# Output projection of a mixer layer: six of its eight weight blocks computed beside the attention units and stored as partial sums

## The chip, the cores and the metric

The kernel runs on one core of one Trainium2 chip. The metric is the device time of one execution in microseconds; the kernel before took 2520.68 us (median of three runs, 2518.25 to 2520.77). The profiled execution is another one and took 2515.9 us.

## The reference

One layer of a hybrid trunk for 2048 prompt rows and 64 sample rows (T = 2112 rows of 1024 numbers). Four mixers A to D give 256 columns each. Their outputs are normalised, scaled, projected by `w_out`, gated by `g1` and added to `x`; then come a second norm and a mixture of experts. What the change touches is this part:

```python
mix = jnp.concatenate([out_a, out_b, out_c, out_d], axis=-1).reshape(Bn, L, N_MIXERS, W_GRP)
mix = (mix * lax.rsqrt(jnp.mean(mix * mix, axis=-1, keepdims=True) + EPS)).reshape(Bn, L, D) * p['out_norm']
x = x + (g1 * (mix @ p['w_out']))
h2 = _rms(x, p['norm_ffn']) * (1.0 + sc2) + sh2
x = x + (g2 * _moe(h2, p))
```

`out_d` is the attention of the prompt (two patterns whose results are merged by a softmax of their maxima and sums) and of the samples; `out_a` to `out_c` are finished earlier and lie, normalised and turned, in `mix_d`. `w_out` has eight blocks of 128 rows: blocks 0 to 5 belong to A to C, blocks 6 and 7 to D. `g1` is one row for the whole prompt and one row for each of the eight samples.

## The kernel before, in words

All engines walk one list, `SCHEDULE`; each engine has a function for some of the step names and executes them in the order of the list. Rows are taken in 17 tiles of 128 (the last has the 64 sample rows).

**The first part** (to 796 us) computes the norms, the input projection, mixers A to C, and q, k and v. A barrier, `("bar", 1)`, ends it.

**The attention units.** There are 128 units: 32 blocks of queries times four heads. `BLOCKS` goes by chunks of 512 rows: for each chunk 16 units of the band pattern (two key blocks of 128; the very first query block has one) and 16 of the dilated one (1, 2, 3 and 4 key blocks in chunks 0 to 3). That is 284 key blocks in all. Slot u of the list holds, in this order (`unit`): `ao` of u-3 (DVE copies a finished block), at even u the pair `au` of u and u+1 (TensorE scores, line 2230, DVE maximum, line 1715, ACT exponential, line 1159), `at` of u-1 (transposes, line 2238, into bank 2 or 3 by parity, copied by DVE at even and by ACT at odd units), `ap` of u-2 (times v, line 2249). `sample(u)` adds the sample attention (lines 2269 to 2299) beside units 3 to 55; its keys and values come by POOL's queue, lines 833 and 838.

**The row steps.** From slot 48 on each slot u has one step of the row tiles too, `tiles(i, j)` with i = (u-48)//8 - 2 and j = (u-48)%8, so that the first projection stands beside unit 64 and the tiles run on after unit 127. A tile has eight such steps:

```python
out = [[("pe", i - 1, 1), ("x", i - 1), ("m1", i + 1)],
       [("m2", i + 1), ("l", i - 2), ("mx", i + 1), ("xt", i)],
       [("m3", i + 1)],
       [("n3", i - 1)],
       [("pe", i, 0), ("ma", i + 2), ("st", i - 1)],
       [("mo", i + 1)],
       [("t", i - 1, 0)],
       [("t", i - 1, 1)]][j]
out = [("p", i, j // 4, j % 4)] + out
```

`p` is a quarter of half a projection: two matmuls of 128x512 (line 2326, bank 5 or 6), 16 to a tile. `pe` (DVE, line 1830) multiplies the half by the gate, `x` adds the input row (DVE, 1836) and squares the sum for the second norm (ACT, 1214 to 1216), `n3` norms it (DVE, 1845 and 1846), `t` turns it (TensorE 2336, ACT 1222), `l` gives the router's logits (2344, 2345). `m1`, `m2` and `m3` merge the two patterns for the tile ahead and norm it (DVE 1785 to 1820, with an exponential on ACT, 1188, between m1 and m2, and a root on ACT, 1194, between m2 and m3); `mo` turns the merged rows. SP's queue loads `mx` (mix_d), `xt` (x) and `ma` (att_d) and stores `st`. Router steps r0 to r4 (DVE mostly) run for four tiles at a time, each batch in the slots `ROUTE` gives; POOL then scatters the rows' places (line 881, ten of them after the last two batches).

**The experts** follow (`moe`): 32 experts' weights come by SP's queue, 2 MB each for `wg`, `wu` and `wd`. Expert 0 is loaded in step `pre` at tile 9, expert 1 in step `w1` after the last tile.

## Time and profile before

| what | value |
| --- | --- |
| median of three runs | 2520.68 us |
| the profiled execution | 2515.9 us, its span 2514.2 us |
| TensorE busy | 2240.9 us (89%) |
| DVE, ACT, POOL busy | 852.5, 550.3, 286.1 us |
| mean granted clock of TensorE | 0.933 of full |

### The profile page before, as it was taken

Reading aid. Unit: us, or ns where it says so; the run is one execution under the profiler, and the core shown is the slowest. Engines: PE = TensorE matmul, PEld = TensorE weight load, DVE = VectorE, ACT = ScalarE, POOL = GpSimd, SP = SyncE. Lnnn points to the kernel's source line nnn. Section 1 sums busy time; section 2 is a strip of 40 time slices with the busy share of each in tenths; the row PEclk is TensorE's granted clock in tenths of the full one; section 3 lists DMA queues with packets and bytes.
Section 4 is the critical chain, followed back from the end, with each engine's and each line's share of the span. In section 5 each row is a group of like instructions: output and inputs, shape, how many; then the busy total and the mean of one; then the engine's idle time right before and its main releaser. Section 6 shows DMA issues by size and latency. Waiting matters only on the chain. (4 is left out here: it accounts for less than half of the span.)

```text
span 2514.2 us, 27705 instructions
## 1 busy us (share of the span) xinstructions
PE 2240.9 (89%) x7615; PEld 1121.0 (45%) x7616; DVE 852.5 (34%) x1969; ACT 550.3 (22%) x1061; POOL 286.1 (11%) x460
## 2 busy tenths in 40 slices
PE   4996999998895778999999849999999999999993
PEld 1343555444452444555554424444444444444441
DVE  4575642036541233445466431111111111111211
ACT  3410101235531322333322201111111111111111
POOL 0001011000001000000021121111111111111211
PEclk8998999999997777999999969999999999999997
DMA  9152131333547424222163245675658789687962
GB/s 378 71 214 48 57 86 48 140 101 99 169 144 242 158 108 174 67 78 85 61 233 131 81 163 156 216 275 170 211 190 326 260 329 343 206 307 278 323 200 59
DMA packets 106523, 438.90 MB, mean 175 GB/s; under 512 B 14955, under 2 KB 53579, under 8 KB 85883
## 3 DMA queue, kind: packets, MB, share of 16 engines
q1 hardware_dynamic: 76160, 309.46, 32.9%
q0 software_dynamic: 26160, 113.16, 16.5%
q10 hardware_dynamic: 4112, 15.14, 1.5%
q8 instruction: 48, 0.79, 0.1%
q14 instruction: 43, 0.35, 0.0%
HBM read 356.39 MB, written 83.10 MB: 175 GB/s over the span
## 5 line engine op out<-in xcount | busy, mean ns | idle before, releaser
L2410 PE MATMUL bank<-arena 128*128 128x512 f32 x1120 | 492.8, 596 | 14.6 <-issue 14.5
L2098 PE MATMUL bank<-arena 128*128 128x512 f32 (+1 forms) x960 | 358.3, 533 | 9.6 <-ACTq L1003 9.6
L2410 PEld LDWEIGHTS bank<-arena 128*128 128x128 f32 x1120 | 212.4, 190 | 291.0 <-issue 291.0
L2326 PE MATMUL bank<-arena 128*128 128x512 f32 (+1 forms) x544 | 267.8, 626 | 0.0
L2438 PE MATMUL bank<-arena 128*128 128x512 f32 x560 | 250.4, 600 | 9.0 <-issue 8.8
L2098 PEld LDWEIGHTS bank<-arena 128*128 128x128 f32 x960 | 168.5, 191 | 193.5 <-issue 192.8
L1990 DVE COPY arena<-bank 128x512 f32<-128x512 f32 x50 | 34.6, 693 | 549.1 <-PE bank L2425 549.1
L2438 PEld LDWEIGHTS bank<-arena 128*128 128x128 f32 x560 | 103.6, 190 | 133.0 <-issue 129.9
L2326 PEld LDWEIGHTS bank<-arena 128*128 128x128 f32 (+1 forms) x544 | 97.5, 195 | 88.4 <-issue 87.9
L2249 PE MATMUL bank<-arena 128*128 128x64 f32 x568 | 95.6, 302 | 31.1 <-DVEq L1733 17.3
L2198 PE MATMUL bank<-arena 128*128 128x512 f32 (+1 forms) x272 | 121.6, 600 | 0.0
L2000 DVE TENSOR_TENSOR arena<-bank,arena 128x512 f32<-128x512 f32 (+1 forms) x50 | 34.5, 691 | 255.9 <-PE bank L2438 208.2
L916 POOL DMA_INDIRECT o_y<-arena x50 | 79.3, 1586 | 301.3 <-DVE arena L2002 215.1
L1715 DVE CUSTOM_DVE_ANT_0 arena<-bank,arena 128x256 f32<-128x256 f32 (+3 forms) x128 | 58.3, 455 | 159.6 <-PE bank L2230 126.3
L1159 ACT ACTIVATE arena<-arena 128x256 f32<-128x256 f32 (+3 forms) x128 | 68.3, 533 | 201.5 <-DVEq L1717 193.6
L2249 PEld LDWEIGHTS bank<-arena 128*128 128x128 f32 x568 | 87.3, 222 | 44.0 <-ACTq L1170 23.3
L2414 PE MATMUL bank<-arena 128*64 128x512 f32 x224 | 99.2, 594 | 6.1 <-issue 5.3
L2415 PE MATMUL bank<-arena 128*64 128x512 f32 x224 | 99.3, 595 | 0.0
L1255 ACT COPY arena<-bank 128x512 f32<-128x512 f32 x52 | 30.6, 588 | 305.3 <-PE bank L2376 305.3
L1041 ACT COPY arena<-bank 128x512 f32<-128x512 f32 (+1 forms) x50 | 25.6, 513 | 314.8 <-PE bank L2098 314.6
L2230 PE MATMUL bank<-arena 64*128 64x256 f32 (+3 forms) x256 | 72.4, 648 | 9.2 <-SPq L440 9.2
L2238 PE MATMUL bank<-arena 128*128 128x128 f32 x284 | 64.4, 321 | 15.2 <-ACTq L1161 15.1
(453 smaller groups left out, 2502.5 us busy)
## 6 DMA issues: line engine op xcount, KB each, us to landing
arena<-wg SPq DMA_DIRECT2D x32, 2048.0 KB
arena<-wu SPq DMA_DIRECT2D x32, 2048.0 KB, 15.1
arena<-wd SPq DMA_DIRECT2D x32, 2048.0 KB, 8.4
arena<-mod_w SPq DMA_DIRECT2D x12, 2048.0 KB, 18.1
z_d<-arena ACTq DMA_DIRECT2D x12, 1056.0 KB, 6.6
arena<-z_d POOLq DMA_DIRECT2D x10, 1056.0 KB, 8.3
arena<-kc POOLq DMA_DIRECT2D x8, 1280.0 KB, 7.6
arena<-vc POOLq DMA_DIRECT2D x8, 1280.0 KB, 8.1
```

The source lines that it names most:

```text
L916: pool.indirect_dma_start(out=O["y"], out_offset=bass.IndirectOffsetOnAxis(ap=sidx[:, s:s + 1], axis=0), in_=yb[:, s], in_offset=None, com ...
L1159: link(act.activation(ssb[:, u % 4, 0:w], ssb[:, u % 4, 0:w], ACT.Exp, bias=ost[:, (u // 4) % 2, u % 4, 64:65], scale=-1.0, accum_out=ost[ ...
L2098: ins = mm(bank[n % 2][:, 0:w], wz[:, i % 3, k, :], hT[:, k, t0:t0 + w], start=(k == 0), stop=(k == KT - 1))
L2198: mm(bank[i % 3][0:r], hT[:, k, t0:t0 + r], wqkv[:, k, 0:512], start=(k == 0), stop=(k == KT - 1))
L2230: mm(bank[u % 2][:, 0:128 * len(vt)], qkT[rr, h // 2, q], qkT[rr, 2 + h // 2, k], start=True, stop=True).then_inc(S("att_s"), 1)
L2238: ins = pe.transpose(bank[2 + u % 2][:, c * P:(c + 1) * P], ssb[:, u % 4, c * P:(c + 1) * P], ident)
L2249: ins = mm(bank[4][:, 64 * h:64 * h + 64], pt[:, u % 4, c * P:(c + 1) * P], v[:, t, 64 * h:64 * h + 64], start=(c == 0), stop=(c == len(vt ...
L2326: ins = mm(bank[5 + q][0:r], l, wo[:, k, 512 * q:512 * q + 512], start=(k == 0), stop=(k == KT - 1))
L2410: ins = mm(bank[bk][:, :], xgT[:, s, k, :], m[w][:, k, :], start=(k == 0), stop=(k == KT - 1))
L2414: gate = mm(bank[2][HIGH, :], xgT[:, s, k, LOW], wg[w][:, k, :], start=(k == 0), stop=(k == KT - 1), tile_position=(0, HB))
L2415: rise = mm(bank[3][LOW, :], xgT[:, s, k, LOW], wu[w][:, k, :], start=(k == 0), stop=(k == KT - 1), tile_position=(0, 0))
L2438: ins = mm(bank[4 + h][:, :], hhT[:, k, :], wd[w][:, k, 512 * h:512 * h + 512], start=(k == 0), stop=(k == 3))
```

## The change

`w_out`'s blocks 0 to 5 leave the row tiles. They become 34 "parts": for each half q of the columns (512) and each of the 17 row tiles, one chain of six matmuls into bank 3 (`part`, two halves of three matmuls, `("w", n, 0)` and `("w", n, 1)`), beside units 2 and 3, 6 to 37, 42 and 43, 46 to 77. Six blocks of weights (`WB`, 256 KB each) are loaded for q = 0 and again for q = 1. DVE scales them by the prompt's gate (`part_scale`, six operations of 128x512) after the sample part has used them unscaled, and adds the part to the row of x that SP has loaded (`part_add`, one operation of 128x512). SP stores the sum to `xp_d` and reads it back in `xt` in x's place. The transposes of units below 80 have bank 2 alone, so that each waits for the copy of the one before.

The row tiles start at unit 78, two steps to a slot while units are left (53 slots), one after that. A tile's projection keeps two matmuls to a half, with a weight scaled beforehand by the gate (`w2g`), and stands at j = 3 and j = 7. DVE takes bank times the row's root plus the stored row in one operation for each half; `x`'s addition and `m3` are gone, and the merged rows' square sum goes from DVE to ACT. The sample rows are tile 1 now instead of tile 16. `pre` stands at (12, 1) instead of (9, 5), and expert 1's `wu` is loaded only when all scatters have landed.

```diff
+        WFIRST = 2
+        ONEBANK = 80
...
+        NW = 2 * NT
+        WAT = [WFIRST + 40 * q + (2 * p + 2 if p else 0) for q in range(2) for p in range(NT)]
...
+        def later(u):
+            out = [("we", n) for n in range(NW) if WAT[n] + 2 == u]
+            return out + [("wsc", n // NT) for f, n in out if n % NT == 0]
+
+        def partial(u):
+            out = []
+            for n in range(NW):
+                if u in (WAT[n], WAT[n] + 1):
+                    out.append(("w", n, u - WAT[n]))
+                if u == WAT[n] and n + 1 < NW and n:
+                    out.append(("wl", n + 1))
+                if u == WAT[n] + 3:
+                    out.append(("wst", n))
+                    out += [("wi", m) for m in range(4, len(WITEMS)) if XI[n] <= m - 4 and (n + 1 == NW or m - 4 < XI[n + 1])]
+                if n == NT - 1 and u == WAT[n] + 2:
+                    out.append(("ww", 1))
+            return out
+
         def unit(u):
-            pair = [("au", u), ("au", u + 1)] if u % 2 == 0 else []
+            pair = [("au", u), *((f, n) for f, n in later(u)), ("au", u + 1)] if u % 2 == 0 else []
...
-                   [("m2", i + 1), ("l", i - 2), ("mx", i + 1), ("xt", i)],
-                   [("m3", i + 1)],
+                   [("m2", i + 1), ("l", i - 2), ("xt", i)],
+                   [],
...
-            out = [("p", i, j // 4, j % 4)] + out
...
+            out = ([("p", i, j // 4)] if j % 4 == 3 else []) + out
...
-            if (i, j) == (9, 5):
+            if (i, j) == (12, 1):
                 out.append(("pre",))
...
-        FIRST_ROW = 48
-        for u in range(FIRST_ROW + 8 * (NT + 4)):
-            i, j = divmod(u - FIRST_ROW, 8)
-            SCHEDULE += unit(u) + sample(u) + (tiles(i - 2, j) if i >= 0 else [])
+        FIRST_ROW = max(WAT) + 2
+        BOTH = NU + 3 - FIRST_ROW
+        for u in range(NU + 3 + 8 * (NT + 4) - 2 * BOTH):
+            SCHEDULE += unit(u) + sample(u) + partial(u)
+            n = u - FIRST_ROW
+            for g in (2 * n, 2 * n + 1) if n < BOTH else (n + BOTH,):
+                if g >= 0:
+                    SCHEDULE += tiles(g // 8 - 2, g % 8)
...
+            return bank[2 + u % 2 if u >= ONEBANK else 2][:, 0:w]
...
+                if m >= 4:
+                    f4, n4 = WITEMS[m - 4]
+                    if f4 == "x":
+                        sp.wait_ge(S(f"st_wx{m % 4}"), 16 * sum(1 for e in range(m % 4, m - 3, 4) if WITEMS[e][0] == "x"))
...
+            def part_out(step, n):
+                r, t0, m = w_rows(n), w_at(n), XI[n]
+                sp.wait_ge(S("w_out"), n + 1)
+                sp.dma_start(xp_d[t0:t0 + r, 512 * (n // NT):512 * (n // NT) + 512], xw[0:r, m % 4]).then_inc(S(f"st_wx{m % 4}"), 16)
...
-                sp.dma_start(xt[0:r, i % 2], A["x"][t0:t0 + r]).then_inc(S(f"ld_xt{i % 2}"), 16)
+                sp.dma_start(xt[0:r, i % 2], xp_d[t0:t0 + r]).then_inc(S(f"ld_xt{i % 2}"), 16)
...
+                sp.wait_ge(S("st_tok"), 16 * 2 * NT)
+                weights_of(1, None, ("wu",))
...
+                    link(TT(x, bank[3][0:r], x, ALU.add))
+                    dve.sem_inc(S("w_free"), 1)
...
-                link(TT(x1[0:r, i % 2, c], bank[5 + q][0:r], g[0:r, 0, c], ALU.mult))
+                    link(STT(y, bank[5 + q][0:r], rstd, x, ALU.mult, ALU.add))
...
-            def x1_sum(step, i):
...
-                link(TT(x1[0:r, i % 2], x1[0:r, i % 2], xt[0:r, i % 2], ALU.add))
...
+                if 0 < u <= ONEBANK:
+                    pe.wait_ge(S("att_ptV" if u % 2 else "att_ptA"), (u - 1) // 2 + 1)
...
+            def part(step, n, half):
+                r = w_rows(n)
+                if half == 0:
+                    pe.wait_ge(S(f"ld_mix{n % 2}"), 16 * (n // 2 + 1))
+                    if n:
+                        pe.wait_ge(S("w_free"), n)
...
+                    ins = mm(bank[3][0:r], mixl[:, n % 2, k, 0:r], WB[k], start=(k == 0), stop=(k == 5))
```

**TensorE beside unit 18 to 21, before.** Scores (2230), transposes (2238), times v (2249) and the samples' values (2297):

```order
L2230 MATMUL bank0<-arena 128x128
L2230 MATMUL bank1<-arena 128x128
L2238 MATMUL bank3<-arena 128x128
L2249 MATMUL bank4<-arena 128x64
L2297 MATMUL bank7<-arena 32x256 x8
L2238 MATMUL bank2<-arena 128x128
L2249 MATMUL bank4<-arena 128x64
L2297 MATMUL bank7<-arena 32x256 x8
```

The same place of the changed kernel (scores 2360, transposes 2372, times v 2383, samples 2431, parts 2458):

```order
L2360 MATMUL bank0<-arena 128x128
L2360 MATMUL bank1<-arena 128x128
L2372 MATMUL bank2<-arena 128x128
L2383 MATMUL bank4<-arena 128x64
L2431 MATMUL bank7<-arena 32x256 x8
L2458 MATMUL bank3<-arena 128x512 x3
L2372 MATMUL bank2<-arena 128x128
L2383 MATMUL bank4<-arena 128x64
L2431 MATMUL bank7<-arena 32x256 x8
L2458 MATMUL bank3<-arena 128x512 x3
```

Each unit has got three matmuls of 512 columns behind its own work, and both transposes go to bank 2.

**TensorE in the row tiles beside units of three key blocks, before.** One projection step (2326) to a unit, here with `mo` (2310) and `t` (2336):

```order
L2230 MATMUL bank0<-arena 128x384
L2230 MATMUL bank1<-arena 128x384
L2238 MATMUL bank3<-arena 128x128 x3
L2249 MATMUL bank4<-arena 128x64 x3
L2326 MATMUL bank6<-arena 128x512 x2
L2238 MATMUL bank2<-arena 128x128 x3
L2249 MATMUL bank4<-arena 128x64 x3
L2326 MATMUL bank6<-arena 128x512 x2
L2310 MATMUL bank7<-arena 128x128 x2
```

The changed kernel's tiles beside units of two key blocks (projection 2473, `mo` 2444, `t` 2482):

```order
L2473 MATMUL bank5<-arena 128x512 x2
L2360 MATMUL bank0<-arena 128x256
L2360 MATMUL bank1<-arena 128x256
L2372 MATMUL bank3<-arena 128x128 x2
L2383 MATMUL bank4<-arena 128x64 x2
L2444 MATMUL bank7<-arena 128x128 x2
L2372 MATMUL bank2<-arena 128x128 x2
L2383 MATMUL bank4<-arena 128x64 x2
L2482 MATMUL bank7<-arena 128x128 x4
L2473 MATMUL bank6<-arena 128x512 x2
L2482 MATMUL bank7<-arena 128x128 x4
```

A tile's projection is four matmuls instead of sixteen, and a tile passes in four units instead of eight.

**DVE in a row tile after the last unit, before** (1830 is `pe`, 1836 the addition of x, 1785 to 1787 `m1`):

```order
L1830 TENSOR_TENSOR arena<-bank6,arena 128x512
L1836 TENSOR_TENSOR arena<-arena 128x1024
L1785 TENSOR_TENSOR arena<-arena 128x4
L1786 TENSOR_TENSOR arena<-arena 128x4
L1787 TENSOR_TENSOR arena<-arena 128x4
```

The changed kernel's DVE in such a tile (1964 is `pe`, 1922 to 1924 `m1`, then the end of `m2`, and `n3` at 1975 and 1976):

```order
L1964 SCALAR_TENSOR_TENSOR arena<-bank6,arena 128x512
L1922 TENSOR_TENSOR arena<-arena 128x4
L1923 TENSOR_TENSOR arena<-arena 128x4
L1924 TENSOR_TENSOR arena<-arena 128x4
L1936 TENSOR_TENSOR arena<-arena 128x4
L1937 TENSOR_TENSOR arena<-arena 128x4
L1938 TENSOR_TENSOR arena<-arena 128x4
L1939 RECIPROCAL arena<-arena 128x4
```

```order
L1943 TENSOR_TENSOR arena<-arena 128x256
L1944 TENSOR_TENSOR arena<-arena 128x256
L1945 TENSOR_TENSOR arena<-arena 128x256
L1975 SCALAR_TENSOR_TENSOR arena<-arena 128x1024
L1976 TENSOR_TENSOR arena<-arena 128x1024
```

`m1` follows `pe` at once, and `n3` follows `m2` at once: the addition of 128x1024 and the norm that stood between `m2` and `n3` (1812, 1820) are gone.

## Rows read from the trace of the kernel before

**Rows 1.** The profile's page: span, and the granted clock in 40 slices.
```profile
span 2514.2 us, 27705 instructions
...
PEclk8998999999997777999999969999999999999997
```
**Rows 2.** Busy time by stretch: length, PE, PEld, DVE, ACT, POOL; then clock, DMA share, GB/s.
```profile
796.00:997.00 201.00, 146.29 (x772) 83.33 (x772) 61.53 (x216) 55.86 (x177) 25.10 (x48) 0.71 0.45 165
997.00:1262.00 265.00, 255.82 (x1108) 148.15 (x1109) 125.74 (x339) 92.87 (x254) 0.28 (x1) 0.94 0.21 73
1262.00:1430.00 168.00, 159.87 (x543) 81.60 (x542) 103.16 (x300) 38.82 (x108) 30.96 (x39) 0.97 0.44 155
1430.00:1486.00 56.00, 11.56 (x66) 9.55 (x67) 31.37 (x133) 6.78 (x19) 13.90 (x19) 0.53 0.52 180
```
**Rows 3.** Timeline of PE around unit 78: start, length, instruction, count, idle before.
```profile
1048.56 0.70 PE L2230 MATMUL bank<-arena 64*128 64x256 f32 x4
```
**Rows 4.** Timeline of PE in a row tile after the last unit.
```profile
1361.57 1.87 PE L2344 MATMUL bank<-arena 128*128 128x36 f32 x16
...
1363.71 7.13 PE L2326 MATMUL bank<-arena 128*128 128x512 f32 x16
1370.68 0.38 PE L2310 MATMUL bank<-arena 128*128 128x128 f32 x2
```
**Rows 5.** Timeline of PE over two units of two key blocks.
```profile
1145.36 0.70 PE L2230 MATMUL bank<-arena 64*128 64x256 f32 x4
...
1148.43 0.60 PE L2336 MATMUL bank<-arena 128*128 128x128 f32 x4
1148.87 0.38 PE L2238 MATMUL bank<-arena 128*128 128x128 f32 x2
...
1151.78 0.70 PE L2230 MATMUL bank<-arena 64*128 64x256 f32 x4
```
**Rows 6.** Groups of PE between 796 and 997: busy, mean ns, idle before.
```profile
L2269 PE MATMUL bank<-arena 128*32 128x512 f32 (+1 forms) x96 | 25.9, 670 | 11.4 <-issue 11.4
L2297 PE MATMUL bank<-arena 128*32 128x256 f32 x160 | 24.3, 450 | 6.2 <-DMA arena<-o_v 6.2
L2282 PE MATMUL bank<-arena 128*128 128x128 f32 x20 | 4.8, 377 | 0.0
```
**Rows 7.** Timeline at the start of the units: POOL and PE.
```profile
805.36 1.07 POOL L833 DMA_DIRECT2D arena<-kc  x2
...
815.24 3.63 PE L2269 MATMUL bank<-arena 128*32 128x512 f32 x8 [8.87 <-issue]
```
**Rows 8.** Timeline of DVE and ACT in a row tile after the last unit.
```profile
1357.90 0.69 DVE L1830 TENSOR_TENSOR arena<-bank,arena 128x512 f32<-128x512 f32 x1 [5.02 <-PE bank L2326]
1358.74 1.23 DVE L1836 TENSOR_TENSOR arena<-arena 128x1024 f32<-128x1024 f32 x1
1360.06 1.06 ACT L1214 ACTIVATE arena<-arena 128x1024 f32<-128x1024 f32 x1 [1.14 <-DVEq L1837]
1361.89 0.21 ACT L1188 ACTIVATE arena<-arena 128x8 f32<-128x8 f32 x1
1362.25 0.17 DVE L1799 TENSOR_TENSOR arena<-arena 128x4 f32<-128x4 f32 x1 [1.57 <-ACTq L1189]
1364.85 0.43 DVE L1812 CUSTOM_DVE_ANT_0 arena<-arena 128x256 f32<-128x256 f32 x1
1368.87 1.29 DVE L1845 SCALAR_TENSOR_TENSOR arena<-arena 128x1024 f32<-128x1024 f32 x1
1370.19 1.23 DVE L1846 TENSOR_TENSOR arena<-arena 128x1024 f32<-128x1024 f32 x1
```
**Rows 9.** Busy time by stretch again: row loads, and expert 0's weights.
```profile
1358.00:1364.00 6.00, 6.00 (x30) 3.99 (x29) 3.83 (x13) 2.45 (x6) 0.00 (x0) 1.00 0.60 199
1300.00:1320.00 20.00, 19.91 (x72) 10.49 (x70) 13.84 (x39) 5.05 (x13) 3.98 (x4) 1.00 1.01 402
```
**Rows 10.** DMA issues by line: KB each, median us to landing.
```profile
o_y<-arena SPq DMA_DIRECT2D x17, 512.0 KB, 2.7
```

305 lines of the change are left out of this document (196 added, 109 removed).

## The prediction

> **What bounds the kernel now.** I read the page first [rows 1]: one core, and TensorE's clock in forty slices. It is at 0.7 in four of them, and these lie beside the attention units. The busy times by stretch say what happens there [rows 2]. From 796 to 997 us stand units 0 to 63 alone: TensorE works 146 of 201 us, at a mean clock of 0.71, so it is neither full nor fast. From 997 to 1262 units 64 to 127 have row steps beside them, and TensorE is busy 256 of 265 us at 0.94. From 1262 to 1430 the row tiles are alone: 160 of 168 us at 0.97. The 56 us to 1486 are the router's last steps and the first gather, and TensorE works 12 of them. So TensorE bounds the two middle stretches, waits on the units' chain in the first, and what can be won is the first stretch's idle time and half clock. The rest of the kernel is not touched.
>
> **Prices, all at full clock.** Eight matmuls of 512 columns take from 1363.71 to 1370.68 [rows 4], so 0.87 us each. Two units of two key blocks with two row steps between take 6.42 us, 1145.36 to 1151.78; the steps are four such matmuls (3.48) and eight transposes (0.44 for four, 1148.43 to 1148.87) [rows 5]; 2.06 us are left, 0.515 to a key block. Of the 284 key blocks 136 belong to units 0 to 77 (70 us) and 148 to units 78 to 127 (76 us). The samples' three large groups are busy 55 us at a clock of 0.71 [rows 6, 2], so 39 us at full clock. A row tile is 16 matmuls (13.9), logits (2.1, 1361.57 to 1363.71 [rows 4]) and ten transposes (1.1): 17.1 us. The new tile has four matmuls: 6.7 us. As a check on such sums, 997 to 1262 holds 176 key blocks and 8.4 tiles, 91 + 144 = 235 us, and took 265: 0.47 us above the sum for each of its 64 units, half of it clock.
>
> **First stretch, units 0 to 77.** TensorE's work adds up to 204 matmuls x 0.87 = 178 us of parts, 70 of units and 39 of samples: 287 us. The waits per unit lie nearest to those of the stretch that also has matmuls beside units, so 78 x 0.47 = 37 us. At the start TensorE waits for the first keys, issued at 805.36 and used at 815.24 [rows 7]; of those 19 us since 796 the first four units and part 0 fill 9; SP's first loads (2.9 MB, 7 us at the 402 GB/s of [rows 9]) go partly ahead of the keys, 3 more: 13 us, and 2 for a spot named below, 15. The stretch ends at 796 + 287 + 37 + 15 = 1135, where unit 78 starts at 1048.56 now [rows 3]. Bounds: 1100 with no waits at all, 1170 with 1 us more for each part. DVE's 34 additions of 0.69 us and twelve scalings (0.69 each, the price of a 128x512 operation [rows 8]) are 32 us on an engine that was busy 62 of 201 us; they lie beside TensorE's work, except that TensorE may not begin a part before the last one's addition is read, which is in the 0.47. The part's matmuls also cover the chain score, maximum, exponential, transpose: 2.6 us of them stand between two units' transposes, and with one bank for these ACT's copy must be over before the next. Without a part in the slot (units 38 to 41, 44, 45) that cover is gone, up to 2 us a pair; before, all pairs went without it, so I add only 2 in all.
>
> **Second stretch, 53 slots with two row steps each.** TensorE has 76 us of units and 11.25 tiles x 6.7 = 75 us. With 0.47 us a slot that is 176 us. DVE is now as loaded: today's tile costs it 1.4 for two gates, 1.23 for the sum, 0.6 for `m1` (three like 1362.25), 2.6 for `m2` (1362.25 to 1364.85), 0.95 for square sum and norm, and 2.55 for `n3` (1368.87 to 1371.42): 9.3 us [rows 8]; 8.4 of these leave 48 of its 126 us [rows 2] for 64 units, 0.75 each. After the change a tile costs it 7.2 us, and 53 x 0.75 + 11.25 x 7.2 plus two batches of router steps (23: what 8.6 tiles of 9.3 leave of the 103 us in the stretch from 1262 [rows 2], which holds two) plus 4 for the gates is 148 us against TensorE's 151. Two engines so alike, each waiting on the other in order, do not reach 176. The other end is today's pace, 265 / 64 = 4.14 us a slot: 219 us. I take the middle, 197: the stretch ends at 1332.
>
> **Third stretch, tiles alone.** 46 steps are left up to the last projection, 5.75 tiles. TensorE would need 6.7 us a tile; what sets the pace is the ring through DVE and ACT: `pe` 0.75, ACT's turn with a copy ahead 0.4, squares and exponential to DVE's next 2.2 (1360.06 to 1362.25), `m2` 2.6, `n3` 2.55 [rows 8], hand-over 0.3, four transposes and the half projection behind them 2.5 [rows 4, 5]: 11.3 us. TensorE then works six tenths of the time. In the stretch where it worked 146 of 201 us the clock was 0.71 [rows 2]; at half clock the last term doubles and the ring is 13.6 us. I take 12.5 as the middle, 72 us. By the Trainium skill (TensorE: Matmul & The Clock Gate, "A second HAM failure mode: psum-queue depth-cycling"), small idle gaps between groups of matmuls make the clock go to and fro between its two rates; with the half rate held throughout, this stretch would be 78 us, with the full rate 65. The row just named agrees with such a to and fro. Router batch 2 adds about 11 us on DVE, 8 of them in the ring. Expert 0's 6.3 MB at 402 GB/s [rows 9] take 16 us of SP's queue; behind them the next merge rows have some 12 steps before they are due, so I add 3. Third stretch: 83 us, bounds 65 + 8 and 78 + 11 + 15.
>
> **The end.** 1332 + 83 = 1415 against 1430. The 56 us to 1486 lose the addition of 1.23 us [rows 8], and gain up to 5 us because expert 1's `wu` now loads together with the token table and the first gathers; expert 1 is wanted a good 20 us later, so only the contention counts: +1 net. The experts stay. In sum -14 us on the profiled execution of 2515.9 us, whose time is 4.8 us below the median of the runs shown: 2502 there, **2507 us** on the median's scale.
>
> **Rivals.**
> **Saturated.** The parts cover every wait of the units and keep the clock at 1.0, and DVE keeps up. Then the first stretch ends at 1118 (half the waits), the second takes 176 and the third 73: 1367, 63 us less than 1430, so 2459. For it: 256 of 265 us busy in the stretch that looks most like it. Against: 30 us were lost there even so, and DVE carries more per slot now.
> **DVE holds the tiles (slower).** A whole tile's DVE work falls into four units instead of eight: in the slot with `pe`, `m1` and `m2` DVE has 4.1 + 0.75 us against TensorE's 3.3, and the maximum of the next pair waits behind `n3`; so exponential, transposes and TensorE wait. Place: units 78 to 127 and every tile after. Price: the second stretch at today's 4.14 us a slot is 219, the third at the half-clock ring 78 + 11 + 8 = 97: 1135 + 219 + 97 = 1451, +21 and +2 at the end: 2543. It decides from the point where the two stretches together pass 1430 - 1135 = 295 us; my sum has 280. For it: the 148 against 151 above. Against: ACT has room (93 of 265 us), and the first eight slots have no projection.
> **Parts come late (slower).** SP stores a part, must see it landed before it loads that buffer's next x, and then comes to the next mixer rows. A store of 512 KB lands after 2.7 us [rows 10]; the row loads moved 1.2 MB in some 5 us [rows 9], so a mixer load of 384 KB lands about 4 us after its issue. Both fit in a part's 8.3 us. But 16 loads of 1.28 MB for the samples go through the same engines, 3 us each. One microsecond on each of 34 parts gives +34 - 14: 2541. By the Trainium skill (DMA: Bandwidth & Descriptors, "Anatomy of one DMA"), most of a transfer's fixed time of about 2 us is the wait for the last byte to be confirmed, longest when it goes to HBM; that speaks against partial sums that are stored and read back, and would cost 34 x 2 = 68 us if SP's queue were full. The store row agrees with the size; nothing in the trace before shows SP full.
> **Nothing in sum.** What the first stretch wins (the 1.0 clock and the filled gaps) the tiles give back within 5 us: 2516 to 2526, which my sum reaches if each of the three stretches is a few us longer. It is part of the first case below.
>
> **How the numbers follow.** My sum as it stands, scattering from 2490 to 2525: 0.42, of which 0.33 below 2515.6 and 0.09 within 0.2% (5 us, about what can be told from no change). Saturated 0.15, faster. DVE holds the tiles 0.24: 0.22 slower, 0.02 within. Parts late 0.13: 0.11 slower, 0.02 within. Smaller mixtures 0.06: 0.02 faster, 0.01 within, 0.03 slower. Faster 0.50, same 0.14, slower 0.36. The likeliest case alone spans 2490 to 2525; with both signs open the range runs from near the saturated case to the slower ones, 2465 to 2545.
>
> **What would show it.** Unit 78's scores should start at 1120 to 1150, with a clock above 0.9 from 830 on; if they start past 1165, look for TensorE waiting at a part's first matmul for a load (parts late) or at a transpose. The last unit should end at 1320 to 1345, the last projection at 1405 to 1430. DVE should be busy about three quarters of the second stretch; if TensorE's waits there name DVE's maximum or copies and a slot takes over 4 us, the DVE rival holds. In the third stretch a tile should take 12 to 13 us at a clock of 0.6 to 0.9; under 9 us would refute the ring. The stretch from the last projection to the experts should stay at 55 to 60 us. I am wrong if the tiles' stretch is shorter than TensorE's work makes it, or the first stretch keeps its 0.71.

## The result and the profile after

The changed kernel takes 2651.84 us (median of 4 runs, 2643.14 to 2652.59), against 2519.80 for the kernel before (2518.25 to 2520.77): 1.052 of it, 95% interval 1.0494 to 1.0539, so 132 us slower. The forecast was 2507, with a range up to 2545, and the chance for slower 0.36. The profiled execution has a span of 2650.9 us against 2514.2. The page, with the line that answers to [rows 1]:

```profile
span 2650.9 us, 28015 instructions
...
PE 2292.4 (86%) x7615; PEld 1144.4 (43%) x7616; DVE 858.0 (32%) x1956; ACT 558.5 (21%) x1095; POOL 285.4 (11%) x466
...
PEclk8998999999986998996777677999999999999997
```

The low clock has moved. Before, four slices at 0.7 lay in the units without row steps; now, behind a first slice of 0.6, the units with parts beside them run at 0.8 to 0.9, and six slices of 0.6 and 0.7 lie where the row tiles are, which were at 0.9.

The busy times by stretch, columns as in [rows 2], this time cut at the units. The kernel before: up to unit 4, units 4 to 77, units 78 to 127 (to the last one's scores), from there to the last projection.

```profile
796.00:819.00 23.00, 7.39 (x25) 3.08 (x26) 3.07 (x15) 3.26 (x10) 11.92 (x23) 0.50 0.84 278
819.00:1049.00 230.00, 185.99 (x923) 105.29 (x923) 82.20 (x276) 67.77 (x215) 13.18 (x25) 0.77 0.35 130
1049.00:1249.00 200.00, 195.74 (x868) 114.83 (x866) 97.17 (x252) 71.59 (x194) 0.00 (x0) 0.96 0.22 76
1249.00:1429.00 180.00, 171.87 (x609) 89.69 (x606) 107.99 (x310) 44.93 (x122) 31.25 (x39) 0.97 0.43 150
```

The same four stretches of the changed kernel, and the one from the last projection to the experts:

```profile
793.00:836.00 43.00, 12.98 (x35) 4.57 (x35) 3.07 (x15) 3.53 (x10) 11.87 (x23) 0.56 0.82 224
836.00:1196.00 360.00, 314.45 (x1256) 154.00 (x1255) 96.94 (x271) 62.14 (x197) 11.06 (x21) 0.93 0.44 141
1196.00:1451.00 255.00, 200.43 (x830) 125.67 (x832) 128.73 (x356) 92.67 (x261) 16.96 (x33) 0.73 0.28 93
1451.00:1560.00 109.00, 81.75 (x301) 50.18 (x299) 68.32 (x202) 37.52 (x105) 16.47 (x16) 0.70 0.44 161
1560.00:1619.00 59.00, 14.41 (x67) 11.59 (x65) 30.23 (x129) 6.68 (x19) 13.45 (x19) 0.54 0.52 192
```

Each length can be split in three: TensorE's work (its busy time times the clock), what the half clock adds to it (the rest of the busy time), and its idle time.

- Units 4 to 77: from 143 work + 43 clock + 44 idle to 292 + 22 + 46. Work +149, time **+130**.
- Unit 78 to the last projection, two stretches together: from 355 + 13 + 12 = 380 to 203 + 82 + 79, 364 (idle 82, clock 79, each rounded). Work **-152**, time **-16**.
- The first four units +20; the rest of the kernel within 6 us (the units start 3 us earlier; from the last projection to the end it is 1091 us against 1085).

So the change did what it says: 150 us of matmuls left the row stretches and went beside the units. They cost nearly their full time where they came to and gave back a tenth of it where they left. Two questions follow: why did the row stretches not shrink, and why did the parts not hide?

What TensorE waits for in units 0 to 77 of the changed kernel (us in total, times, longest):

```profile
PE bank L2458 <- DMA arena<-mix_d: 25.9, 1, 25.9
PE bank L2458 <- DVEq L1849: 20.8, 21, 1.3
PE bank L2372 <- ACTq L1274: 19.1, 4, 8.4
```

L2458 is a part's first matmul. Once it waits for the first mixer rows, and 21 times for VectorE's addition of the part before. The timeline shows how the latter comes about, at 928 us:

```profile
927.67 0.83 PE L2360 MATMUL bank<-arena 64*128 64x128 f32 x4
...
928.64 0.29 DVE L1823 CUSTOM_DVE_ANT_0 arena<-bank,arena 128x128 f32<-128x128 f32 x1 [2.81 <-PE bank L2360]
...
929.17 0.69 DVE L1848 TENSOR_TENSOR arena<-bank,arena 128x512 f32<-128x512 f32 x1 [0.22 <-DVE arena L1823]
...
930.06 4.51 PE L2458 MATMUL bank<-arena 128*128 128x512 f32 x6 [1.13 <-DVEq L1849]
930.21 0.29 DVE L1823 CUSTOM_DVE_ANT_0 arena<-bank,arena 128x128 f32<-128x128 f32 x1 [0.35 <-DVE arena L1848]
```

The addition (L1848) could have been done from 927.7 on, but it stands behind the unit's maximum (L1823), which waited 2.81 us for the next scores. So TensorE waits 1.13 us with the next half part, and its three matmuls (six records) run mostly at half clock: 4.51 us, where the three before them took 2.80.

The third row of the waits is the single bank for the transposes: four times, 19.1 us in all, TensorE could not start a transpose before ScalarE's copy of the one before it. In the kernel before no transpose of these units waits for a copy.

In the row stretches, a tile beside four units, between its norm (L1975) and the next one's, at 1315 us:

```profile
1315.04 1.28 DVE L1975 SCALAR_TENSOR_TENSOR arena<-arena 128x1024 f32<-128x1024 f32 x1 [0.50 <-DVE arena L1833]
...
1317.88 0.43 DVE L1823 CUSTOM_DVE_ANT_0 arena<-bank,arena 128x256 f32<-128x256 f32 x1 [0.29 <-DVE arena L1976]
...
1318.41 0.51 ACT L1263 ACTIVATE arena<-arena 128x256 f32<-128x256 f32 x1 [3.04 <-DVEq L1825]
...
1319.11 0.69 PE L2372 MATMUL bank<-arena 128*128 128x128 f32 x2 [3.14 <-ACTq L1265]
...
1322.29 3.62 PE L2473 MATMUL bank<-arena 128*128 128x512 f32 x4
...
1326.48 0.70 PE L2360 MATMUL bank<-arena 64*128 64x256 f32 x4
...
1327.33 0.43 DVE L1823 CUSTOM_DVE_ANT_0 arena<-bank,arena 128x256 f32<-128x256 f32 x1 [5.38 <-PE bank L2360]
...
1332.11 0.17 DVE L1936 TENSOR_TENSOR arena<-arena 128x4 f32<-128x4 f32 x1 [1.95 <-ACTq L1293]
...
1335.43 0.66 PE L2383 MATMUL bank<-arena 128*128 128x64 f32 x4 [1.85 <-DVEq L1834]
1335.47 1.29 DVE L1975 SCALAR_TENSOR_TENSOR arena<-arena 128x1024 f32<-128x1024 f32 x1
```

The unit's maximum stands behind the norm's two passes; the exponential waits 3.04 us for it, and TensorE 3.14 for the exponential. Then come the turn of h2 and a projection half at half clock, 3.62 us for two matmuls (four records, L2473), which take 1.9 at 1330.64. Behind them stand the next scores, and VectorE waits 5.38 us for these. ScalarE takes part as well: in the row at 1332.11 VectorE's merge waits 1.95 us for ScalarE's exponential, which stands behind the squares of the tile before. So in each tile TensorE waits for VectorE and VectorE for TensorE, and neither is busy: of the 20.5 us TensorE 14.7 and VectorE 9.9.

```profile
1315.00:1335.50 20.50, 14.69 (x68) 9.28 (x67) 9.85 (x28) 7.87 (x24) 0.00 (x0) 0.75 0.27 98
```

The tiles alone, the same periods from 1464.5 on:

```profile
1464.50:1483.40 18.90, 13.62 (x42) 9.36 (x43) 15.69 (x54) 5.44 (x17) 0.00 (x0) 0.59 0.30 105
1483.40:1497.00 13.60, 11.72 (x37) 6.61 (x36) 7.13 (x17) 4.15 (x11) 8.23 (x8) 0.63 0.75 264
1497.00:1517.00 20.00, 13.46 (x40) 6.70 (x38) 8.43 (x27) 6.52 (x21) 0.00 (x0) 0.59 0.79 322
1517.00:1535.60 18.60, 11.91 (x37) 8.15 (x38) 15.33 (x54) 5.19 (x16) 0.00 (x0) 0.59 0.28 100
1535.60:1547.20 11.60, 9.72 (x37) 5.39 (x37) 6.81 (x16) 3.77 (x9) 8.24 (x8) 0.79 0.43 137
```

The second and the last hold no router steps and take 13.6 us at a mean clock of 0.63 and 11.6 at 0.79. The first and fourth hold a router batch; VectorE is busy 15 to 16 of 19 us, so the tile is little longer than its queue. In the third VectorE waits once, 4.7 us, for the merge rows.

### The profile page after: what moved, and what is told of

Same layout as the page of the kernel before. It is cut to its first block and busy times, and to the rows that moved or that the text cites. A ratio compares the mean times of both kernels' runs of the same rounds, so it can differ in the third digit from the quotient of the medians.

```text
span 2650.9 us, 28015 instructions
## 1 busy us (share of the span) xinstructions
PE 2292.4 (86%) x7615; PEld 1144.4 (43%) x7616; DVE 858.0 (32%) x1956; ACT 558.5 (21%) x1095; POOL 285.4 (11%) x466
## 5 line engine op out<-in xcount | busy, mean ns | idle before, releaser
L2228 PE MATMUL bank<-arena 128*128 128x512 f32 (+1 forms) x960 | 359.1, 534 | 9.6 <-ACTq L1107 9.6
L2458 PE MATMUL bank<-arena 128*128 128x512 f32 (+1 forms) x408 | 204.2, 638 | 46.7 <-DMA arena<-mix_d 25.9
L2458 PEld LDWEIGHTS bank<-arena 128*128 128x128 f32 (+1 forms) x408 | 74.2, 195 | 133.4 <-issue 107.1
L1823 DVE CUSTOM_DVE_ANT_0 arena<-bank,arena 128x256 f32<-128x256 f32 (+3 forms) x128 | 58.3, 455 | 219.7 <-PE bank L2360 195.1
L2328 PE MATMUL bank<-arena 128*128 128x512 f32 (+1 forms) x272 | 119.9, 593 | 0.0
L2383 PE MATMUL bank<-arena 128*128 128x64 f32 x568 | 96.5, 306 | 25.2 <-ACTq L1274 10.0
L2560 PE MATMUL bank<-arena 128*64 128x512 f32 x224 | 102.6, 611 | 6.5 <-issue 5.6
L2383 PEld LDWEIGHTS bank<-arena 128*128 128x128 f32 x568 | 90.3, 230 | 35.3 <-ACTq L1274 15.2
L2561 PE MATMUL bank<-arena 128*64 128x512 f32 x224 | 102.7, 611 | 0.0
L2473 PE MATMUL bank<-arena 128*128 128x512 f32 (+1 forms) x136 | 101.3, 887 | 0.0
```

Of the source, the lines that this page charges most:

```text
L2228: ins = mm(bank[n % 2][:, 0:w], wz[:, i % 3, k, :], hT[:, k, t0:t0 + w], start=(k == 0), stop=(k == KT - 1))
L2328: mm(bank[i % 3][0:r], hT[:, k, t0:t0 + r], wqkv[:, k, 0:512], start=(k == 0), stop=(k == KT - 1))
L2383: ins = mm(bank[4][:, 64 * h:64 * h + 64], pt[:, u % 4, c * P:(c + 1) * P], v[:, t, 64 * h:64 * h + 64], start=(c == 0), stop=(c == len(vt ...
L2458: ins = mm(bank[3][0:r], mixl[:, n % 2, k, 0:r], WB[k], start=(k == 0), stop=(k == 5))
L2473: ins = mm(bank[5 + q][0:r], odt[:, i % 2, k, 0:r], w[:, k, 512 * q:512 * q + 512], start=(k == 0), stop=(k == 1))
L2560: gate = mm(bank[2][HIGH, :], xgT[:, s, k, LOW], wg[w][:, k, :], start=(k == 0), stop=(k == KT - 1), tile_position=(0, HB))
```

## Experiments

All kernels were timed against the kernel before on the same chip. Times are medians in us; the changed kernel is 2652, and a difference "in the changed kernel" is taken from that. The groups of experiments ran on different chips, on which the kernel before took 2518.5 to 2520.2, and the executions of one kernel lie up to 20 us apart. So a difference of 8 us or less to the changed kernel is not told from none; nor is one of some 7 us in a single stretch, for the units 4 to 77 in their unchanged order took 353 to 360 us (experiments 3, 4, 5, 6, 16 and the changed kernel).

**1 and 2: the units' chain.** If TensorE waits in the row stretches for a unit's scores, maximum and exponential, one more slot between them should help.

```
-  [("ao", u - 3), *pair, ("at", u - 1), ("ap", u - 2)]
+  [("ao", u - 4), *pair, ("at", u - 2), ("ap", u - 3)]
```

> The changed kernel with the attention units' transposes, value products and outputs one slot later (transposes two slots after the scores, not one). Theory CHAIN (TensorE waits in units 78 to 130 for the unit's own chain scores, maximum, exponential, now held up by two tile steps on VectorE and ScalarE): the waits of the transposes go, 40 to 55 us of idle and part of the 53 us lost at half clock in that stretch; the kernel falls from 2652 to 2560 to 2610. Theory CLOCK (too little TensorE work in a slot, the waits are only where the slack collects): the waits move to the value products or scores, 2635 to 2655. Theory QUEUE (VectorE's and ScalarE's total work per slot sets the pace): under 15 us of gain, 2637 to 2655.

> The same one-slot delay of transposes, value products and outputs, in the kernel before. CHAIN says that the matmuls of the row tiles already covered this latency from unit 64 on, so that only units 0 to 60 gain (their 72 us of idle between 796 and 1430 at most): 2490 to 2520. CLOCK and QUEUE: 2515 to 2525.

Measured: 2656.0 (+4, no clear difference) in the changed kernel, 2529.1 (+9; ratio 1.0025 to 1.0064) in the one before. The gain that CHAIN forecast did not come, but the edit moved the wait instead of taking it away. Between units 78 and 127 TensorE's waits at the transposes for the exponential fell from 26.4 to 2.4 us, and this took their place (waits from 1188 to 1450, then the timeline):

```profile
PE bank L2383 <- DVEq L1866: 55.7, 10, 7.5
...
1335.98 0.42 DVE L1865 COPY arena<-bank 128x256 f32<-128x256 f32 x1
...
1336.61 1.09 PE L2383 MATMUL bank<-arena 128*128 128x64 f32 x4 [5.28 <-DVEq L1866]
```

Once a tile the product with v (L2383) now waits for VectorE's copy of a finished block (L1865), which with the delay stands right behind the merge in VectorE's order. So the experiment refutes the gain, not the kind of wait: TensorE still waits for what stands behind a tile step in VectorE's queue.

**3: more work for TensorE.** Three thrown-away matmuls ahead of each projection half.

```
+  for k in range(3):
+      mm(bank[5 + q][0:r], odt[:, i % 2, 0, 0:r], w[:, 0, 512 * q:512 * q + 512], start=True, stop=True)
```

> The changed kernel with three more matmuls (128x128 by 512, result overwritten by the half's own product) ahead of each half of the two-block projection: 34 x 3 = 102 matmuls, 22 us at full clock and 44 us at half. CLOCK (the granted clock falls for want of TensorE work): the clock in stretches 2 and 3 rises and pays for them, total change between -30 and +5 us. CHAIN (latency on VectorE and ScalarE sets the pace, matmuls stand beside it): they fall into TensorE's idle time, change between -5 and +15. If TensorE's own work is the bound, +22 to +45.

The size in that expectation was wrong: 102 matmuls at 0.87 us [rows 4] are 89 us, not 22. Measured 2694.7, +43. By stretch (units 78 to 127, tiles alone):

```profile
1191.00:1475.00 284.00, 242.36 (x951) 142.48 (x952) 128.65 (x356) 93.23 (x262) 17.00 (x33) 0.83 0.25 84
1475.00:1603.00 128.00, 107.09 (x385) 61.41 (x382) 68.25 (x202) 37.06 (x105) 16.51 (x16) 0.88 0.38 142
```

Against the changed kernel the clock rose from 0.73 and 0.70, and the work of 89 us cost 48 in these stretches. Nearly half of it was free: neither "TensorE is the bound" nor "all hidden".

**4: one tile step a slot.** The doubling undone (`BOTH = 0`).

> The changed kernel with one tile step a slot from unit 78 on, not two. CHAIN and QUEUE (the doubled tile steps hold up the units' maximum and exponential): units 78 to 130 fall from 4.9 us a slot to 3.7 to 4.2 (196 to 222 us instead of 259), and the 53 steps left over then run alone, 6.6 tiles at 18.8 us = 125 more; sum +62 to +88, 2715 to 2740. If the units' own chain sets the pace whatever the tiles do, the slot stays at 4.6 to 4.9 us and the sum is +110 to +125, 2760 to 2775.

Measured 2658.7, +7, not told from none. Units 78 to 127 fell from 255 to 178 us, 3.6 a slot, and the tiles alone needed 201 us instead of 109. So 50 steps, taken out of the units' slots, saved 77 us there (1.5 each) and cost 92 alone (1.8 each). The doubling isn't the loss, and it gains little either: beside a unit a step costs five sixths of what it costs alone.

**5 and 8: the circle opened.** In a tile the order closes a circle: norm of tile i-1, its turn on TensorE, behind it the second projection half of tile i, its gate, squares, then the norm of tile i. Here the second half stands ahead of the turn:

```
-  out = [[("pe", i - 1, 1), ("x", i - 1), ("m1", i + 1)],
+  out = [[("m1", i + 1)],
...
-         [("t", i - 1, 0)],
+         [("pe", i, 1), ("x", i), ("t", i - 1, 0)],
...
-  out = ([("p", i, j // 4)] if j % 4 == 3 else []) + out
+  out = ([("p", i, j // 4)] if j in (3, 5) else []) + out
```

> The changed kernel with a tile's second projection half ahead of the turning of h2 of the tile before (steps 3 and 5 of the eight, gate and squares at step 6), so that the circle norm's scale and shift, turn, projection half, gate, squares, next norm no longer closes through TensorE's order. Theory RING (this circle, with the units' and the routing's work standing in the same queues, sets the pace of units 78 to 130 at 19.6 us a tile and of the tiles alone at 18.8): a tile falls towards VectorE's own 13 to 15 us; units 78 to 130 from 255 to 190 to 220 us, the tiles alone from 109 to 75 to 90; kernel 2560 to 2610. Theory VECTOR (VectorE's instructions in a row, circle or not): 2630 to 2650. Theory UNITS (the units' chain): 2635 to 2655.

> The opened circle and the units' transposes one slot later, together. RING: with the circle gone the unit's own chain comes next, so the delay that gave nothing alone now gives 5 to 25 us over the opened circle alone. VECTOR: nothing over it.

Measured 2644.9 (-7; ratio to the kernel before 1.0482 to 1.0534, where the changed kernel has 1.0494 to 1.0539, so not told from none) and, with the later transposes, 2667.0 (+15). The units 78 to 127 took 237 us instead of 255, the tiles alone 116 instead of 109. RING fell as the sole cause, for it forecast 2560 to 2610. TensorE now waits elsewhere in the tile: 43.2 us in 15 waits between the two turnings of h2, for ScalarE's copy of the first, which stands behind the squares.

**6 and 7: more work for VectorE.** Three passes of 128x256 to scratch in each tile's merge, in both kernels.

```
+  for _ in range(3):
+      link(TT(osq, o, o, ALU.mult))
```

> The changed kernel with three more 128x256 passes on VectorE (0.43 to 0.46 us each, written to scratch) at the end of the merge of each of 16 tiles: 22 us more of VectorE's work. RING and VECTOR: all of it stands on the path in both row stretches, +18 to +24 (2670 to 2676). CLOCK or UNITS: VectorE is busy for 45% of these stretches, so it is hidden, 0 to +6.

> The same 22 us of VectorE's work in the kernel before. RING and VECTOR say that there 18.3 us of TensorE's work a tile (14.3 of them the projection) covered a circle of nearly the same length, so between 0 and +8: 2520 to 2528. If VectorE had slack of several us a tile, 0 to +2.

Measured +23 (2675.1) in the changed kernel and **+25** (2543.9, ratio 1.0070 to 1.0117) in the one before, of 22 us added. The second was a surprise: there TensorE is busy 196 of 200 and 172 of 180 us, and still each microsecond of VectorE's work in a tile costs one. Its units 78 to 127 with the passes, against 200 us, 0.96 without:

```profile
1055.00:1270.00 215.00, 204.59 (x868) 119.61 (x870) 104.88 (x270) 71.90 (x194) 0.00 (x0) 0.91 0.21 71
```

Split as above, the 200 us were 188 of work, 8 of half clock and 4 of idle time, and the 215 are 186, 18 and 10. So of the 15 us in this stretch some 10 are half clock and 6 are waits. VectorE's order was on the path here too, under a TensorE busy for 98% of the time, and the gaps that it makes in TensorE's work come with more half clock. That this is the circle of experiment 5 is not shown.

**9: a third of each part.** Two of six matmuls kept (mixer blocks 1 to 4 of 0 to 5 are left out of y).

```
-  for k in range(3 * half, 3 * half + 3):
+  for k in ((0,), (5,))[half]:
```

> The changed kernel with two of the six matmuls of each of the 34 partial sums (left out: mixer blocks 1 to 4, so the rows of y miss them). 136 matmuls of 0.87 us at full clock, 118 us of work, are gone from units 2 to 77. If TensorE's own work sets the pace there, units 4 to 77 fall by about 118 (360 to 242) and the kernel to about 2535. If the units' own chain has a floor of 3.0 to 3.2 us a unit, as the kernel before shows without tiles, they fall only to 235 to 260 and waits and half clock come back; either way the stretches behind unit 78 stay as they are (364 us).

Measured 2571.9: -80 for 118 us of matmuls. Units 4 to 77, and the two row stretches, unchanged as both readings said:

```profile
837.00:1125.00 288.00, 213.96 (x990) 106.41 (x989) 96.87 (x271) 62.13 (x197) 11.05 (x21) 0.88 0.55 176
1125.00:1379.00 254.00, 199.27 (x829) 125.29 (x828) 128.65 (x356) 92.66 (x261) 16.97 (x33) 0.74 0.27 92
1379.00:1489.00 110.00, 82.29 (x304) 50.93 (x303) 68.28 (x202) 37.52 (x105) 16.48 (x16) 0.71 0.44 162
```

The 288 us lie over both expected values. In the emptier slots (two executions, one profile) TensorE waits 38 us in 30 waits at its transposes for ScalarE's copy out of the single bank, and still 18.7 us in 19 waits for the part's addition.

**10: a late start alone.** The kernel before with its row steps from slot 78 on (`FIRST_ROW = 78`).

> The kernel before with its row steps from slot 78 on, not 48, nothing else changed (whole projection in the tile, one step a slot). Thirty steps leave the units' slots and run alone at the end, 3.75 tiles at 19.5 us = 73 us more, and the units that they leave get shorter by 0.8 to 1.0 us a slot, 24 to 30 us: +43 to +50, 2563 to 2570. If a late start alone were what the change loses, the kernel would come near 2650.

Measured 2542.8, +23 (ratio 1.0064 to 1.0118). That is about a sixth of the loss. The 30 steps that left the units' slots took 44 us with them (units 4 to 77 took 209 us, units 78 to 127 took 177), where I gave 24 to 30; the tiles alone took 242 us instead of 180.

**11: lighter on VectorE, in the kernel before.** If experiment 7 holds downward too, taking work off VectorE should pay there.

```
-  link(TT(w1, e1, m[:, 0, :, 65], ALU.mult))
-  link(TT(w2, e2, m[:, 1, :, 65], ALU.mult))
+  link(TT(mw[:, 7:9], mw[:, 4:6], m[:, :, :, 65], ALU.mult))
...
-  link(dve.tensor_tensor_reduce(out=osq[0:r], in0=o, in1=o, scale=1.0, scalar=0.0, op0=ALU.mult, op1=ALU.add, accum_out=ss))
...
+  link(act.activation(spt[0:r, 0:2].rearrange("p n m -> p (n m)"), od[0:r, i % 2], ACT.Square, accum_out=mw[0:r, 9, 0:1]))
...
+  link(act.activation(od[0:r, i % 2], od[0:r, i % 2], ACT.Copy, scale=mw[0:r, 9, 0:1]))
```

> The kernel before with less on VectorE in each tile's merge: three pairs of small passes made one each (0.2 us each), and the sum of squares and the normalisation of the merged row done by ScalarE (0.51 and 0.36 us and a round trip less on VectorE): 1.4 to 1.5 us a tile off VectorE, 22 to 24 us in all. VECTOR (each us of VectorE's work in a tile costs one, also in the kernel before, as run e7 showed upward): 15 to 24 us faster, 2495 to 2505. If TensorE's work is now the bound when VectorE is relieved: 0 to 5 us faster, 2514 to 2520.

Measured **2507.9** (2505.6 to 2509.7), ratio 0.9941 to 0.9969: the fastest version, and it beats both kernels. Its units 78 to 127:

```profile
1046.00:1238.00 192.00, 188.75 (x868) 109.97 (x870) 89.56 (x216) 77.82 (x211) 0.00 (x0) 1.00 0.23 79
```

200 us became 192 at full clock, with TensorE busy 189; the 8 us are the half clock that was left there. The tiles alone gained nothing, 183 us against 180, though VectorE was busy 98 us instead of 108; ScalarE was busy 53 instead of 45. VectorE's work fell by some 21 us in all, the time by 12: beside the units the slope ends at TensorE's own work, and why it ends in the tiles alone is not shown.

**12: three mends of the changed kernel.** The circle opened, the three merged passes of 11, and a part's addition ahead of the maxima:

```
-  pair = [("au", u), *((f, n) for f, n in later(u)), ("au", u + 1)] if u % 2 == 0 else []
+  pair = [*((f, n) for f, n in later(u)), ("au", u), ("au", u + 1)] if u % 2 == 0 else []
```

> The changed kernel with three edits together: the circle opened as in e5, the three small passes merged (0.6 us a tile, 10 us), and a part's addition put ahead of the units' maxima on VectorE. VECTOR: 2645 minus 10 for the passes minus 10 to 20 in the units 2 to 77 (where a part's first matmul waits 21 us in all for that addition): 2610 to 2630. If the waits on the addition only move to the units' own chain: 2630 to 2640.

Measured 2620.2, -32. Units 4 to 77 fell from 360 to 327 us (from 353 to 360, by the scatter named above), and the waits at a part's first matmul from 20.8 us to nothing:

```profile
840.00:1167.00 327.00, 303.70 (x1254) 149.91 (x1253) 96.94 (x271) 62.19 (x197) 11.05 (x21) 0.95 0.49 156
...
PE bank L2455 <- DVEq L1849: 0.3, 1, 0.3
```

The merged passes gave nothing in the row stretches (238 and 116 us, 237 and 116 in experiment 5), so with the circle open 8 us less of VectorE's work no longer counts there. TensorE waits 44.1 us in 15 waits between the two turnings of h2, as in experiment 5.

**13: the single transposition bank alone,** in the kernel before up to unit 79.

> The kernel before with the units' transposes in one bank up to unit 79 (a transpose waits for the copy of the unit before), nothing else. In e9, where little else stands in the units' slots, the transposes wait 43 us in 32 waits for that copy. If the single bank costs this much by itself: units 4 to 77 from 230 to 260 to 275, kernel +25 to +45. If the wait only stands in slack: 0 to +8.

Measured 2526.8, +8 (ratio 1.0009 to 1.0039); units 4 to 77 took 241 us, not 230, and TensorE waited 37.1 us in 29 waits at its transposes for ScalarE's copy. More than half of that took the place of other waits: TensorE was idle for 60 us of the 241, and for 44 of the 230.

**14, 16 and 17: the half clock.** Two thrown-away matmuls ahead of the second turning of h2, on top of experiment 12 (14) and alone (16); with one more in each unit from 80 on (17).

```
+  if q and i + 1 < NT:
+      pe.wait_ge(S("prj_free"), 2 * i + 3)
+      for k in range(2):
+          mm(bank[5][0:P], ident, w2g[:, k, 0:512], start=True, stop=True)
```

> The kernel of e12 with two matmuls (128x128 by 512, result thrown away) ahead of the second turning of h2 in each tile, where TensorE waits 3.2 us a tile for ScalarE's copy: 32 matmuls, 28 us at full clock. If the half clock costs by itself, they fill the wait, raise the clock and pay for themselves: -5 to -20 against e12 (2600 to 2615). If the waits are what costs and the clock stands in their shadow: 0 to +8. If TensorE's order has no real slack there: +14 to +28.

> The changed kernel with the 32 thrown-away matmuls of e14 (28 us at full clock) and nothing else. CLOCK (the half clock costs by itself in the row stretches, about 80 us of the 364): -10 to -25 against 2652 (2627 to 2642). If in this order the projection half already fills the gap, so that they lie on the path: +10 to +28.

> The kernel of e14 with one more matmul (128x128 by 256, 0.44 us at full clock) a unit from unit 80 on, ahead of the wait for the unit's exponential: 48 matmuls, 21 us. In e14 79 of 225 us between units 78 and 127 are still at half clock, 37 us lost, and 28 idle. CLOCK: -5 to -15 against 2596. If what is left at half clock only stands in waits: 0 to +10.

Measured 14: 2596.4, **24 us faster** than 12 for 28 us more work. The two row stretches of 12, then of 14:

```profile
1167.00:1405.00 238.00, 200.40 (x831) 132.10 (x832) 124.62 (x327) 94.77 (x266) 16.98 (x33) 0.72 0.29 99
1405.00:1521.00 116.00, 86.50 (x297) 56.67 (x296) 64.65 (x183) 34.93 (x100) 16.47 (x16) 0.71 0.43 158
```

```profile
1162.00:1388.00 226.00, 197.59 (x867) 122.93 (x868) 124.58 (x327) 94.38 (x265) 16.99 (x33) 0.83 0.31 104
1388.00:1495.00 107.00, 81.20 (x320) 49.05 (x317) 64.23 (x183) 35.31 (x100) 16.48 (x16) 0.84 0.47 172
```

The clock went from 0.72 and 0.71 to 0.83 and 0.84, and TensorE's busy time fell though it did more; its waits between the two turnings fell from 44.1 to 12.0 us. Here the half clock cost by itself. Run 16: 2672.3, +20 against the changed kernel, though its clock rose too, to 0.77 and 0.78: there a projection half already lies in that gap, so the matmuls, it seems, stand on the path. Run 17: 2598.7, against 2596.4 within their scatter, though the clock between units 78 and 127 rose to 0.91. What was left at half clock there cost nothing that more matmuls could win back.

**15: the parts two units later** (`WFIRST = 4`, on top of 12).

> The kernel of e12 with every part two units later (first part beside unit 4, row steps from slot 80). The first part then waits less for its loads, which land 26 us after the start of the units, and two more units run ahead of it (6 to 7 us): the wait falls to 16 to 20 us, the row steps start two slots later (under 2 us by e10): -4 to -10 against e12. If the loads themselves come later because more stands ahead of them: 0 to +3.

Measured 2619.7, no change. The first four units fell from 44 to 30 us; TensorE still waited 17.7 us there, now for the samples' first keys. The tiles alone took 127 us instead of 116: won at the start, given back at the end, where four more steps, half a tile, now run alone.

**18: filling the units' waits in the fastest version.**

> The kernel of e11 (the kernel before, lighter on VectorE) with two thrown-away matmuls (128x128 by 256, 0.44 us each at full clock) in each of units 0 to 63 ahead of the wait for the exponential: 56 us of work where TensorE is idle 44 us and loses 38 at half clock. CLOCK: -5 to -20 against 2508 (2488 to 2503). If the units' chain over VectorE and ScalarE alone sets the pace there: within 3 us. If the matmuls stand on the path: +10 to +40.

Measured 2522.5, 15 us slower than experiment 11. The clock in units 4 to 77 rose from 0.78 to 0.94, their time from 229 to 240 us. Beside units alone a higher clock, bought with 56 us of matmuls, did not pay. How much of the 11 us is the matmuls' own place in the units' chain, and whether the half clock by itself costs anything there, the run cannot tell.

## Why the prediction was wrong

By its own terms, on the profiled execution: the first stretch was to end at 1135 and ended at 1196 (+61); the second, 53 slots, was to take 197 us and took 285 (+88); the third 83, and took 79 (-4). That is 145 of the 151 us by which the profiled execution, forecast at 2502, was missed. The second and third in the forecast's own cut, with the last slot's logits ending at 1481:

```profile
1196.00:1481.00 285.00, 222.86 (x934) 142.16 (x934) 150.08 (x431) 104.85 (x295) 16.96 (x33) 0.73 0.27 91
1481.00:1560.00 79.00, 59.32 (x196) 33.69 (x196) 46.97 (x128) 25.34 (x71) 16.47 (x16) 0.68 0.53 195
```

**"TensorE's work adds up to ... 287 us"**: near. Busy time times clock gives 7 + 292 = 299. The sum was right within 4%.

**"78 x 0.47 = 37 us" of waits and "15 us" at the start**: here 52 us stood for 104, 76 of idle time and 28 of half clock. Two things were wrong. (a) The 0.47 was taken from a stretch whose fillers need nothing from VectorE between them. A part's first matmul does: the text put this "in the 0.47", but by the rows at 928.64 and 929.17 the addition stands behind a maximum that has only just been released. Moving the addition took the 20.8 us of waits away and 26 to 33 us off the stretch, together with part of its half clock (experiment 12; its other two edits only touch row steps). (b) At the start the forecast put the wait on the samples' keys, and the first part waits longer, for the mixer rows:

```profile
793.11 2.96 SPq L711 DMA_DIRECT2D arena<-w_out  x6
793.53 3.09 POOL L928 DMA_DIRECT2D arena<-sk_d  x6 [61.77 <-SPq L488]
...
796.11 0.43 SPq L705 DMA_DIRECT2D arena<-mix_d  x1
...
802.63 1.06 POOL L935 DMA_DIRECT2D arena<-kc  x2
...
825.75 4.53 PE L2458 MATMUL bank<-arena 128*64 128x512 f32 x5 [25.95 <-DMA arena<-mix_d]
```

Part 0 is the 64 sample rows, a load of 192 KB. Issued at 796.11 it was there 29.6 us later, behind six weight loads of 256 KB in its own queue and beside GpSimd's tables, keys and values, all issued within 13 us. The next mixer load, 384 KB issued at 802.76, took 28.6 us. Which of the loads around it held it up was not tested. Part 0 stands beside unit 2 in TensorE's order, so the units behind it waited with it: 43 us instead of 23. Experiment 15 took this wait away, and TensorE waited 17.7 us for the keys instead, twice the 8.9 of the kernel before that the forecast went by.

**"I take the middle, 197"** (second stretch) is the step that failed most. It compared TensorE's 151 us with VectorE's 148 and looked for the time between their totals and today's pace. The totals were right: TensorE's work is 223 x 0.73 = 163 us, VectorE was busy 150. The time, 285, is neither: 62 us are idle and 60 half clock, against 46 allowed (197 less 151). The rows from 1315 on show a chain that runs through TensorE, VectorE and ScalarE in their orders, norm, maximum, exponential, transpose, turn, projection half, scores, maximum, gate, merge, norm, 20.5 us for four units and a tile, of which each engine works a part while the others wait. What the runs show of it is that VectorE's time in a tile is on the path (experiment 6), that opening it at one place brings another wait in its stead (experiments 1 and 5), and that part of the half clock costs by itself (experiment 14). And the upper end, 4.14 us a slot, was no bound, because it was taken from slots with one step, under matmuls that filled the waits. Pricing the steps in a row, as the forecast did for the third stretch, would have been the better bound.

**"11.3 us ... at half clock 13.6. I take 12.5"** (third stretch) was right: tiles without router steps took 11.6 us at 0.79 and 13.6 at 0.63. Router steps made two tiles 19 us, and merge rows that came late one 20; with what the forecast allowed for both (8 and 3) the sum is off by 4. The clock did go to and fro, 3.62 us for two matmuls at 1322.29 and 1.94 for two at 1330.64: the Trainium skill (TensorE: Matmul & The Clock Gate, "A second HAM failure mode: psum-queue depth-cycling"), by which short idle gaps between matmul groups make the rate swing, agrees with that and with experiment 14, where a filled gap raised 0.71 to 0.84. That a higher clock pays, which a reader might take from it, held in experiment 14 and not in 16, 17 and 18. Two figures of the forecast are slips that change nothing: the ring with its last term doubled is 13.8, not 13.6, and the first stretch with half the waits ends at 1116.5, not 1118.

**The rivals.** "DVE holds the tiles" (0.24, 2543) comes nearest to what happened. Its mechanism, "the maximum of the next pair waits behind `n3`; so exponential, transposes and TensorE wait", is to be read in the rows from 1315 on; its condition, the two stretches over 295 us, was met with 364; experiment 6 shows VectorE's work in a tile on the path, +23 for 22. Too small was its price, 219 us for the second stretch, and its reason, a whole tile in four units, was not the point: undone, the kernel gets no faster (experiment 4). Nor is its one place the whole: without the waits for the exponential others of the same kind came (experiment 1). "Parts come late": there was one such wait, 25.9 us, at part 0; behind it no part waits for a load, and the 68 us do not appear that the forecast named for a full SP queue, by the landing time of the Trainium skill (DMA: Bandwidth & Descriptors, "Anatomy of one DMA"); that section describes transfers that GpSimd issues, and these are SP's. "Saturated" is refuted by 0.73 and 0.70 in the row stretches. The end, "+1 net", is 59 us against 57.

**What was not seen in the profile before.** TensorE was busy 196 of 200 and 172 of 180 us in the two row stretches, and the forecast read that as TensorE's bound. Experiment 7 shows that VectorE's order was on the path as well. Taking 152 us of matmuls out of these stretches gave back 16, while putting them beside the units cost 150. Of that 20 went at the beginning and 26 to 33 by the addition's place (experiment 12); a late start of the tiles costs 23 by itself (experiment 10), in the kernel before.

**Still open.** Once the circle is open TensorE waits mostly for ScalarE's copy of the first turning (44.1 us in experiment 12), but whether that copy, the squares ahead of it or the units beside it set the pace was not tried, nor how the 82 us of idle and 79 of half clock divide between the chains: with the edits of experiments 12 and 14 the changed kernel is still 77 us above the one before. Experiment 1 with the block's copy kept ahead of the merge, which would have tried the wait for the exponential alone, was not run. What two banks for the transposes would give beside the parts was not tried, since the parts hold the other bank.

## What to carry to other kernels

Before moving work off an engine that is busy 97% of the time, add a few microseconds to the second engine in the same loop and time it. Here they cost their full length, and the first one's relief bought a tenth of what was taken off. For a loop of in-order queues sum the steps in a row, router-like extras of some rounds included, and not the engines' totals; and put whatever frees a buffer for the busiest engine ahead of work that has yet to wait. Thrown-away matmuls paid in one run of five (experiment 14, not 3, 16, 17 or 18), where TensorE waited once a tile for ScalarE; they raised the granted clock in all five, so the clock alone doesn't tell. And when a wait has been taken away, look in the next trace for where it went: in experiments 1, 5 and 15 another had come in its place.
